# Where the loads of weights are issued: ScalarE beside its cast, or SyncE among the DMA transposes

## The chip, the cores and the metric

One core of one Trainium2 chip runs the kernel. The metric is the device time of one execution in microseconds (us), as the median of several. The engines are TensorE (PE), VectorE (DVE), ScalarE (ACT), GpSimd (POOL) and SyncE (SP); each has its own instruction queue and they meet by semaphores. DMAs are issued by SP, ACT or POOL on a queue of their own and carried out by 16 DMA engines that all of them share.

## The reference

Two layers over 256 tokens of width 1024, in float32:

```python
for l in range(2):
    x = x + 0.5 * swiglu_ffn(rmsnorm(x, norm_ffn1[l]), w_ffn1_in[l], w_ffn1_out[l])   # 2816 hidden
    u = rmsnorm(x, norm_mix[l])
    q, k, v, g, p, c, gates = split(u @ w_in[l])
    y_ret = (retention(q, k, v, positions) * silu(g)) @ w_ret_out[l]
    y_pool = pool_mixer(p, w_pool[l], pool_scale[l])
    y_conv = conv_module(c, ...)            # causal depthwise convolution, 31 taps
    x = x + (sig(g0) * y_ret + sig(g1) * y_pool + sig(g2) * y_conv) @ w_out[l]
    x = x + 0.5 * swiglu_ffn(rmsnorm(x, norm_ffn2[l]), w_ffn2_in[l], w_ffn2_out[l])
return rmsnorm(x, norm_final)
```

## The kernel before

Every product is made of three matmuls on numbers split in two: a high part (`w_hi`, rounded by a cast to fp32r) and a low part (`w_lo`, the rest). The weights come in one stream of 208 **halves** of 128 partitions x 2048 floats (1 MB; a few are smaller), two to a block, 104 to a layer, in the order in which TensorE uses them. For each half: a load into one of `RAWS` = 7 buffers `raw`; ScalarE's cast into one of `HIGHS` = 5 buffers `w_hi` (`cast`, L761 to L771); VectorE's subtraction into `w_lo`, which has the place of `raw` (`sub`, L1167, L1172); then the matmuls. TensorE says when a half is used up (`front_used`, `mm_done`), and `wait_half_used` (L340) waits for that: `cast(hf)` for half hf - 5, the load of hf for half hf - 7. So the load of half hf + 2 waits for the same half as the cast of hf.

SyncE runs one list for all halves (L713 to L735): wait until half hf - 7 is used, issue the load (L717), then, at fixed places, issue DMA transposes: `turn_h` (L672) for the hidden values of a feed-forward block, `turn_x` (L680) for x, `turn_qk` and `turn_ret` (L697) in the mixer. Each first waits for the 16-bit planes that ScalarE splits off (`split_h`, `split_x` L792) and for the buffer. A wait of SyncE holds what stands behind it in the list.

Between the parts lie five **seams** (`seam`, L840 on ScalarE, L1253 on VectorE): into the mixer and into the second feed-forward part of each layer, and into layer 1. There x is turned in four quarters, two for each 128 tokens. A quarter is added up (L1193), split (L796), turned (L684), joined by VectorE (`x_join`, L1210), scaled by ScalarE (`x_high`, L804) and its low part made by VectorE (`x_low`, L1219). ScalarE's order in a seam is: split quarter 1, square, split quarter 2, scale 1, `cast(hf + 1)`, `cast(hf + 2)`, scale 2, split 3, `cast(hf + 3)`, split 4, scale 3, square, scale 4, `cast(hf + 4)`. In the seam into the mixer of layer 0 hf is 34. SyncE has the first two transposes behind load hf + 2, the third behind hf + 3, the fourth behind hf + 4. In a mixer TensorE soon after turns `u` (`turn_u`, L484, L477), which VectorE makes in `gated_u` (L1345, L1348) after `sub` of half hf + 4.

In the mixer ScalarE splits the retention's result (`split_ret`, L936), SyncE turns it, ScalarE puts it together (`ret_out`, L943) and rounds it (`ret_high`), and TensorE waits for `ret_low`.

Of the kernel before, what the change touches and what calls it, by code (L numbers as in the profile page):

```python
# [15 lines left out]
P = 128  # L16
# [29 lines left out]
ALL_HALVES = L * HALVES  # L46
HALF_AT = 2048
HALF = P * HALF_AT
# [10 lines left out]
RAWS = 7  # L59
HIGHS = 5  # L60


FIRST = 4
# [44 lines left out]
def trunk(nc, x_in, positions, weights_in, gate_bias, pool_scale, norm_final, params, ident_in,  # L108
          inv_freq_in, decay_in, band_in, x_first_in, out):
    with ExitStack() as ctx:  # L110
# [3 lines left out]
        def sem(name):  # L114
            return ctx.enter_context(nc.semaphore(name))
# [43 lines left out]
        def place(name, shape, dt=F32):  # L159
            t = nc.alloc_sbuf_tensor_at(name, shape, dt, offset=end[0])  # L160
            end[0] += 4 * int(np.prod(shape[1:]))
            return t

        raw = place("raw", [P, RAWS, HALF_AT])
# [65 lines left out]
        raw_landed = [sem(f"raw_landed{i}") for i in range(RAWS)]  # L230
# [102 lines left out]
        def loads(hf):  # L333

            return hf // RAWS + (hf % RAWS >= FIRST)

        def size(hf):
            return HALF_SIZE[hf // 2 % CHUNKS]

        def wait_half_used(e, hf):  # L340


            l, g, second = hf // HALVES, hf // 2 % CHUNKS, hf % 2
            if g == M_POOL:
                e.wait_ge(mm_done, PRODUCT[l, g, 1, second])
            elif second:
                e.wait_ge(mm_done, PRODUCT[l, g, 1, 1 if (l, g, 1, 1) in PRODUCT else 0])
            else:
                e.wait_ge(front_used, l * (CHUNKS - 1) + g + (g < M_POOL))
# [11 lines left out]
        def wait_tr_taken(e, name):  # L361
            e.wait_ge(tr_taken[TURN[name] % 2], TURN[name] // 2 + 1)

        block = ctx.enter_context(nc.Block())

        @block.tensor
# [304 lines left out]
        def _(sp):  # L671
            def turn_h(l, f, b):  # L672
                at = (2 * l + f) * FB + b
                sp.wait_ge(h_split, T * (at + 1))
                sp.wait_ge(h_whole, at)
                sp.dma_start_transpose(hT_planes[:].rearrange("p a (g n) -> p (a g) n", n=P),
                                       h_planes[:].rearrange("p a k t n -> p (a k t n)")
                                       ).then_inc(h_turned, 16)

            def turn_x(l, norm, t, c):  # L680
                at = piece(l, norm, t, c)
                sp.wait_ge(x_split, at + 1)
                sp.wait_ge(x_joined, at)
                sp.dma_start_transpose(xT_planes[:].rearrange("p a (g n) -> p (a g) n", n=P),  # L684
                                       x_planes.rearrange("p a k n -> p (a k n)")
                                       ).then_inc(x_turned, 16)
# [13 lines left out]
                                       ret_planes[:, t].rearrange("p a h n -> p (a h n)")  # L700
                                       ).then_inc(ret_turned[t], 16)

            def half_in(hf):
                return weights_in[hf * HALF:(hf + 1) * HALF].rearrange("(p n) -> p n", p=P)

            for i in range(QUARTERS):
                s = columns(i % 4)
                sp.dma_start(raw[:, i // 4, s], half_in(i // 4)[:, s]  # L708
# [1 line left out]
            for t in range(T):  # L710
                sp.dma_start(x[:, t, :], x_in.rearrange("a (t p) d -> p (a t) d", p=P)[:, t, :]
                             ).then_inc(x_landed[t], 16)
            for hf in range(FIRST, ALL_HALVES):  # L713
                if hf >= RAWS:
                    wait_half_used(sp, hf - RAWS)
                n = size(hf)
                sp.dma_start(raw[:, hf % RAWS, 0:n], half_in(hf)[:, 0:n]  # L717
                             ).then_inc(raw_landed[hf % RAWS], 16)

                for at, norm in ((0, 0), (MIX, 1), (FFN2, 3)):  # L720
                    if (hf // HALVES, norm) in SEAM:
                        for ahead, t, c in ((2, 0, 0), (2, 0, 1), (3, 1, 0), (4, 1, 1)):
                            if hf % HALVES == 2 * at + ahead:
                                turn_x(hf // HALVES, norm, t, c)

                l, g = hf // HALVES, (hf % HALVES - RAWS - 1) // 2
                for f in (0, 1):
                    if hf % 2 == 0 and f * FFN2 <= g < f * FFN2 + FB:
                        turn_h(l, f, g - f * FFN2)
                for t in range(T):  # L730
                    if hf % HALVES == 2 * M_K + RAWS:
                        turn_qk(l, 0, t)
                    if hf % HALVES == 2 * M_V + RAWS:
                        turn_qk(l, 1, t)
                    if hf % HALVES == 2 * M_POOL + 1 + RAWS:  # L735
                        turn_ret(l, t)
# [7 lines left out]
        def _(act):  # L744
# [16 lines left out]
            def cast(hf):  # L761
                if hf >= ALL_HALVES:
                    return
                n = size(hf)
                act.wait_ge(raw_landed[hf % RAWS], 16 * loads(hf))
                if hf // 2 % CHUNKS == M_POOL:
                    act.wait_ge(pool_scaled, 2 * (hf // HALVES) + hf % 2 + 1)
                if hf >= HIGHS:
                    wait_half_used(act, hf - HIGHS)
                nc.scalar.copy(w_hi[:, hf % HIGHS, 0:n], raw[:, hf % RAWS, 0:n]  # L770
                               ).then_inc(hi_split, 1)  # L771

# [1095 lines left out]
```

## Time and profile before

| | us |
|---|---|
| median of 3 runs (1141.49 to 1142.49) | 1141.62 |
| the profiled execution | 1143.67 |
| its span | 1141.7 |
| busy: PE / DVE / ACT / POOL | 1128.9 / 794.9 / 630.0 / 31.5 |
| share of the span: PE / DVE / ACT | 99% / 70% / 55% |
| a load of 1 MB, issue to landing, median of 192 | 5.0 |
| a DMA transpose of x or the hidden values, issue to landing, median of 64 | 3.1 |

The spans and times below belong to the one profiled execution; the median is that of other executions. "Busy" of PE is modelled, since its matmuls overlap: a matmul of 512 columns is given 0.39 us there and the next one begins 0.23 us after it. The granted clock of TensorE is at full speed in all 40 slices of the page but for short stretches inside them.

### The profile page before, as it was taken

How to read it: one execution, taken by the hardware profiler on the slowest of the kernel's cores; microseconds unless marked ns; L12 is line 12 of the kernel's file. 1: busy time of each engine (PE TensorE's matmuls, PEld its weight loads, DVE VectorE, ACT ScalarE, POOL GpSimd, SP SyncE). 2: the span in 40 equal slices, each digit the busy share in tenths (PEclk: the TensorE clock that was granted, in tenths of full speed). 3: DMA queues.
4: the chain of work that ended last, by engine and by line, in shares of the span. 5: the costliest groups of instructions: out<-in, count | busy, mean ns of one | idle time of the engine just before them, and what ended most of it. 6: DMA issues, size and time to landing. Idle time of an engine off the chain costs nothing.

```text
span 1141.7 us, 13153 instructions
## 1 busy us (share of the span) xinstructions
PE 1128.9 (99%) x5063; PEld 931.9 (82%) x5063; DVE 794.9 (70%) x974; ACT 630.0 (55%) x723; POOL 31.5 (3%) x68
## 2 busy tenths in 40 slices
PE   9999999999999999999999999999999999999997
PEld 6788888788878888888888888878888788888886
DVE  5756565799999766555476656477999986665543
ACT  6755536654555675644465554275637366655442
POOL 1000000000100000000000000000001001000000
PEclk9999999999999999999999999999999999999999
DMA  9976665663764586756587656475637646876541
GB/s 348 324 242 219 211 233 160 239 175 139 243 241 151 164 292 212 238 156 230 174 274 250 236 180 233 176 217 207 212 120 261 233 152 184 273 244 210 168 184 37
DMA packets 116078, 240.99 MB, mean 211 GB/s; under 512 B 84256, under 2 KB 85664, under 8 KB 91440
## 3 DMA queue, kind: packets, MB, share of 16 engines
q1 hardware_dynamic: 112512, 232.28, 60.8%
q0 software_dynamic: 1648, 6.06, 1.5%
q10 hardware_dynamic: 1856, 1.81, 0.5%
q8 instruction: 40, 0.66, 0.2%
q14 instruction: 22, 0.18, 0.0%
HBM read 219.16 MB, written 1.05 MB: 193 GB/s over the span
## 4 chain that ended last, share of the span: by engine, by line
PE 86%; DVE 7%; DMA 2%; ACT 2%; issue 2%; SPq 1%; POOLq 0%; DVEq 0%; POOL 0%; ACTq 0%
PE acc L385 28%; PE acc L387 28%; PE acc L386 28%; DVE w_lo L1172 3%; DVE y L1396 1%; DMA raw<-in_weights 1%; PE tr L477 1%; ACT w_hi L770 1%; DMA hT_planes<-h_planes 1%; SPq L708 1%; ACT pin L945 0%; DVE gates L1471 0%; DVE ua L1452 0%; DVE gates L1416 0%; DVE qk L1461 0%
## 5 line engine op out<-in xcount | busy, mean ns | idle before, releaser
L1172 DVE TENSOR_TENSOR w_lo<-raw,w_hi 128x2048 fp32r<-128x2048 f32 (+2 forms) x204 | 444.4, 2211 | 87.7 <-ACT w_hi L770 87.7
L770 ACT CAST w_hi<-raw 128x2048 fp32r<-128x2048 f32 (+2 forms) x204 | 375.2, 1849 | 230.0 <-PE acc L387 221.8
L385 PE MATMUL acc<-w_hi,xT_hi 128*128 128x512 f32 x1152 | 453.1, 393 | 1.3 <-DVE w_lo L1172 1.1
L387 PE MATMUL acc<-w_hi,xT_lo 128*128 128x512 f32 x1152 | 449.3, 390 | 0.0
L386 PE MATMUL acc<-w_lo,xT_hi 128*128 128x512 f32 x1152 | 449.1, 390 | 0.0
L385 PEld LDWEIGHTS acc<-w_hi,xT_hi 128*128 128x128 f32 x1152 | 216.7, 188 | 46.4 <-DVE w_lo L1172 1.5
L387 PEld LDWEIGHTS acc<-w_hi,xT_lo 128*128 128x128 f32 x1152 | 216.7, 188 | 45.6
L386 PEld LDWEIGHTS acc<-w_lo,xT_hi 128*128 128x128 f32 x1152 | 216.9, 188 | 43.9
L1248 DVE SCALAR_TENSOR_TENSOR h<-acc,rs,silu_gate 128x256 f32<-128x256 f32 x88 | 42.5, 483 | 154.7 <-ACT silu_gate L837 154.4
L385 PE MATMUL acc<-w_hi,hT_hi 128*128 128x512 f32 x348 | 135.4, 389 | 0.0
L386 PE MATMUL acc<-w_lo,hT_hi 128*128 128x512 f32 x348 | 135.4, 389 | 0.0
L387 PE MATMUL acc<-w_hi,hT_lo 128*128 128x512 f32 x348 | 135.4, 389 | 0.0
L837 ACT ACTIVATE silu_gate<-acc,rs 128x256 f32<-128x256 f32 x88 | 41.6, 473 | 103.1 <-PE acc L387 103.1
L1396 DVE SCALAR_TENSOR_TENSOR y<-uT,par,y 128x256 f32<-128x256 f32 x240 | 97.2, 480 | 0.0
L386 PEld LDWEIGHTS acc<-w_lo,hT_hi 128*128 128x128 f32 x348 | 65.3, 188 | 13.7
L385 PEld LDWEIGHTS acc<-w_hi,hT_hi 128*128 128x128 f32 x348 | 65.3, 188 | 13.6
L387 PEld LDWEIGHTS acc<-w_hi,hT_lo 128*128 128x128 f32 x348 | 65.3, 188 | 13.4
L822 ACT COPY h_planes<-h 128x512 uint16<-128x512 uint16 x88 | 50.4, 620 | 8.9 <-DVE h L1248 8.9
L796 ACT COPY h_planes<-x 128x1024 uint16<-128x1024 uint16 x20 | 20.9, 1047 | 39.8 <-DVE x L1193 25.1
L1219 DVE SCALAR_TENSOR_TENSOR xT_lo<-hT_whole,par,xT_hi 128x128 fp32r<-128x128 f32 x80 | 22.7, 346 | 21.3 <-ACT xT_hi L804 21.3
L1231 DVE COPY hT_whole<-hT_planes 128x1024 uint16<-128x1024 uint16 x44 | 33.3, 757 | 5.8 <-DMA hT_planes<-h_planes 5.8
L804 ACT ACTIVATE xT_hi<-hT_whole,par 128x128 fp32r<-128x128 f32 x80 | 25.6, 392 | 15.4 <-DVE hT_whole L1210 15.4
(138 smaller groups left out, 629.4 us busy)
## 6 DMA issues: line engine op xcount, KB each, us to landing
raw<-in_weights SPq DMA_DIRECT2D x192, 1024.0 KB, 5.0
raw<-in_weights SPq DMA_DIRECT2D x20, 256.0 KB, 7.2
raw<-in_weights SPq DMA_DIRECT2D x8, 512.0 KB, 3.5
bias<-in_gate_bias POOLq DMA_DIRECT2D x6, 512.0 KB, 6.5
x<-in_x SPq DMA_DIRECT2D x2, 512.0 KB, 10.7
hT_planes<-h_planes SPq DMA_TRANSPOSE x64, 3.1
scale_row<-in_pool_scale POOLq DMA_DIRECT2D x2, 512.0 KB, 7.7
x_first<-in_x_first ACTq DMA_DIRECT2D x7, 128.0 KB, 6.0
```

What stands on the lines that cost most here:

```text
L385: nc.tensor.matmul(o, a_hi, b_hi, start=first, stop=False)
L386: nc.tensor.matmul(o, a_hi, b_lo, start=False, stop=False)
L387: return nc.tensor.matmul(o, a_lo, b_hi, start=False, stop=last)
L770: nc.scalar.copy(w_hi[:, hf % HIGHS, 0:n], raw[:, hf % RAWS, 0:n]).then_inc(hi_split, 1)
L804: nc.scalar.activation(xT_hi[:, k, tokens(t)], x_whole[:, i, :], ACT.Copy, scale=gain(l, norm, k)).then_inc(x_hi_ready, 1)
L822: nc.scalar.copy(h_planes[:, :, :, t, :], h[:, t, :].bitcast(U16).rearrange("p (k n a) -> p a k n", k=2, a=2)).then_inc(h_split, 1)
L837: nc.scalar.activation(silu_gate[:, t, :], acc[:, t, IN_BANK[g], 0:256], ACT.Silu, scale=rs[:, t:t + 1]).then_inc(silu_ready, 1)
L1172: nc.vector.tensor_tensor(w_lo[:, hf % RAWS, 0:n], raw[:, hf % RAWS, 0:n], w_hi[:, hf % HIGHS, 0:n].bitcast(F32), ALU.subtract).then_inc(l ...
L1219: a = nc.vector.scalar_tensor_tensor(xT_lo[:, k, tokens(t)], x_whole[:, i, :], gain(l, norm, k), xT_hi[:, k, tokens(t)].bitcast(F32), ALU. ...
L1231: nc.vector.tensor_copy(hT_whole[:].rearrange("p k n -> p (k n)").bitcast(U16) .rearrange("p (m a) -> p a m", a=2), hT_planes[:]).then_inc ...
L1248: nc.vector.scalar_tensor_tensor(h[:, t, :], acc[:, t, IN_BANK[g], 256:512], rs[:, t:t + 1], silu_gate[:, t, :], ALU.mult, ALU.mult).then_ ...
L1396: a = nc.vector.scalar_tensor_tensor(y[:, c, :], u, par[:, l, w:w + 1], y[:, c, :], ALU.mult, ALU.add)
```

## The change

ScalarE issues the loads of halves 7 to 207, each in `cast` of the half two before it, between the wait for the used half and the cast. The wait for the used half now stands ahead of those for the landed half and for the scaled pool weights. SyncE keeps the loads of halves 0 to 6, the transposes in their order, and no other wait.

```diff
+        def half_in(hf):
+            return weights_in[hf * HALF:(hf + 1) * HALF].rearrange("(p n) -> p n", p=P)
+
+        def load(e, hf):
+            n = size(hf)
+            e.dma_start(raw[:, hf % RAWS, 0:n], half_in(hf)[:, 0:n]
+                        ).then_inc(raw_landed[hf % RAWS], 16)
+
         block = ctx.enter_context(nc.Block())
...
-            for hf in range(FIRST, ALL_HALVES):
-                if hf >= RAWS:
-                    wait_half_used(sp, hf - RAWS)
-                n = size(hf)
-                sp.dma_start(raw[:, hf % RAWS, 0:n], half_in(hf)[:, 0:n]
-                             ).then_inc(raw_landed[hf % RAWS], 16)
+            for hf in range(FIRST, RAWS):
+                load(sp, hf)
+
+            for hf in range(RAWS, ALL_HALVES):
 
                 for at, norm in ((0, 0), (MIX, 1), (FFN2, 3)):
...
                 n = size(hf)
+                if hf >= HIGHS:
+
+                    wait_half_used(act, hf - HIGHS)
+                    if hf - HIGHS + RAWS < ALL_HALVES:
+                        load(act, hf - HIGHS + RAWS)
                 act.wait_ge(raw_landed[hf % RAWS], 16 * loads(hf))
                 if hf // 2 % CHUNKS == M_POOL:
                     act.wait_ge(pool_scaled, 2 * (hf // HALVES) + hf % 2 + 1)
-                if hf >= HIGHS:
-                    wait_half_used(act, hf - HIGHS)
                 nc.scalar.copy(w_hi[:, hf % HIGHS, 0:n], raw[:, hf % RAWS, 0:n]
                                ).then_inc(hi_split, 1)
```

## Rows read from the trace of the kernel before

**Rows 1.** The page, part 1: busy time, share of the span, instructions.

```profile
PE 1128.9 (99%) x5063; PEld 931.9 (82%) x5063; DVE 794.9 (70%) x974; ACT 630.0 (55%) x723; POOL 31.5 (3%) x68
```

**Rows 2.** Waits of PE: for whom, us in total, times, longest.

```profile
PE tr L477 <- issue: 2.3, 1, 2.3
...
PE acc L385 <- DVE w_lo L1172: 1.1, 1, 1.1
PE tr L477 <- DVE ua L1348: 0.9, 1, 0.9
```

**Rows 3.** The chain of waits in layer 0: start us, us, what.

```profile
203.07 2.29 issue
...
206.04 0.43 PE acc L385
```

**Rows 4.** Timeline of SyncE's queue, seam of layer 0: start, us, instruction.

```profile
176.46 5.40 SPq L684 DMA_TRANSPOSE hT_planes<-h_planes  x2
...
188.55 1.25 SPq L684 DMA_TRANSPOSE hT_planes<-h_planes  x1
...
194.23 1.24 SPq L684 DMA_TRANSPOSE hT_planes<-h_planes  x1
```

**Rows 5.** Timeline of ACT in the same seam, with idle time before.

```profile
181.69 3.70 ACT L770 CAST w_hi<-raw 128x2048 fp32r<-128x2048 f32 x2
...
191.68 1.05 ACT L796 COPY h_planes<-x 128x1024 uint16<-128x1024 uint16 x1 [1.34 <-DMA hT_planes<-h_planes]
...
199.26 1.89 ACT L770 CAST w_hi<-raw 128x2048 fp32r<-128x2048 f32 x1
```

**Rows 6.** Timeline of DVE in the same seam.

```profile
183.91 0.76 DVE L1210 COPY hT_whole<-hT_planes 128x1024 uint16<-128x1024 uint16 x1 [0.95 <-DMA hT_planes<-h_planes]
...
193.41 0.74 DVE L1210 COPY hT_whole<-hT_planes 128x1024 uint16<-128x1024 uint16 x1
...
199.38 1.14 DVE L1219 SCALAR_TENSOR_TENSOR xT_lo<-hT_whole,par,xT_hi 128x128 fp32r<-128x128 f32 x4 [1.35 <-ACT xT_hi L804]
201.18 2.29 DVE L1172 TENSOR_TENSOR w_lo<-raw,w_hi 128x2048 fp32r<-128x2048 f32 x1 [0.66 <-ACT w_hi L770]
```

**Rows 7.** Timeline of ACT and its DMA queue (ACTq) near the start.

```profile
4.57 0.33 ACTq L753 DMA_DIRECT2D x_first<-in_x_first  x1
4.98 0.60 ACT L777 CAST w_hi<-raw 128x512 fp32r<-128x512 f32 x1
```

**Rows 8.** Timeline of SyncE's queue in a feed-forward part.

```profile
114.71 3.05 SPq L717 DMA_DIRECT2D raw<-in_weights  x2
119.97 1.24 SPq L676 DMA_TRANSPOSE hT_planes<-h_planes  x1
```

**Rows 9.** DMA queues, 22 to 26 us (q1 SyncE's, q10 ScalarE's): packets, MB, share.

```profile
q1 hardware_dynamic: 210, 1.51, 90.7%
q10 hardware_dynamic: 209, 0.13, 10.9%
```

**Rows 10.** DMA queues from 121.8 to 122.7 us (q0 is GpSimd's).

```profile
q0 software_dynamic: 88, 0.36, 104.2%
q1 hardware_dynamic: 1, 0.00, 0.1%
```

**Rows 11.** The line of x's transposes (L684, 20 of them).

```profile
DMA to landing us min/median/max: 3.0/3.0/3.3
```

**Rows 12.** Timeline of PE: first matmul on the last quarter of x.

```profile
201.55 0.39 PE L385 MATMUL acc<-w_hi,xT_hi 128*128 128x512 f32 x1
```

**Rows 13.** Timeline of ACT near the start.

```profile
27.71 1.91 ACT L770 CAST w_hi<-raw 128x2048 fp32r<-128x2048 f32 x1 [2.02 <-DMA raw<-in_weights]
```

**Rows 14.** Timeline of SyncE's queue and of ACT, retention transposes of layer 0.

```profile
306.93 5.83 SPq L699 DMA_TRANSPOSE retT_planes<-ret_planes  x2
...
312.81 1.05 SPq L717 DMA_DIRECT2D raw<-in_weights  x2
...
314.64 1.35 ACT L945 COPY pin<-retT_planes 128x1024 uint16<-128x1024 uint16 x1
```

More of the change, by code:

```diff
@@ L701, in turn_ret @@
                                        ).then_inc(ret_turned[t], 16)
-            def half_in(hf):
-                return weights_in[hf * HALF:(hf + 1) * HALF].rearrange("(p n) -> p n", p=P)
             for i in range(QUARTERS):
```

## The prediction

> **What bounds the kernel now.** I read the page first, for the engine that is never idle. TensorE is: busy 99% of the span [rows 1]. Its waits come next, since only what adds to them can cost time and only what they hold can be gained. In all they are a few us [rows 2]: 2.3 before the turning of `u` in layer 0, 0.9 at the same place of layer 1, 1.1 near the start, and, too short for that view, four of 0.2 to 0.3 in the two mixers, where matmul starts lie 0.45 to 0.48 us apart. The chain of waits shows what the first does besides: after 2.29 us without work the matmuls come 0.43 us apart instead of 0.23 (1.2 instead of 2.4 GHz), nine of them [rows 3], which is 9 x 0.2 = 1.8 us. So some 8 us is all that any change to the waits could give back, and the question is what the new order adds.
>
> Then I followed that first wait back through the other engines. `gated_u` waits on VectorE behind `sub` of half 38 (201.18, 2.29 us), that behind ScalarE's cast (199.26), that behind the scaling of the last turned quarter, and so on through the four DMA transposes of the seam [rows 4, 5, 6]. The stretch from 183.91 to 194.15 is VectorE without a hole of more than 0.1 us, and it began when the second transpose landed. So a transpose that lands late moves the end of the kernel, us for us, at the seams that lead into a mixer. That is the place to examine.
>
> **The change part by part.** *Issues on ScalarE.* 201 loads (halves 7 to 207) leave SyncE for ScalarE. One takes 0.33 us of a queue, so 201 x 0.33 = 66 us of ScalarE's sequencer. ScalarE is 55% busy, and the issue does not hold its datapath: the issue at 4.57 stands behind the cast in the program and yet began 0.4 us before that cast ran at 4.98 [rows 7]. Where a copy or an activation is running (the casts at 181.69 and 199.26) the issue lies beneath it: 0 to 0.1 us. Where ScalarE was waiting for the half, the cast comes 0.33 us later; `sub` reads it some 2 to 4 us later in those stretches. I take 0.1 us on the path, at most 0.4. If the cover failed at the two seams, it would be 0.33 at each.
>
> *Time of the loads.* The same half is waited for, so in the feed-forward blocks a load leaves when it does now. There two loads are issued from 114.71 and the transpose only at 119.97, when most of their bytes are in [rows 8]; these blocks keep their distance. At the seams it is otherwise. Now SyncE issues load 37 behind the second transpose, 38 behind the third, 39 behind the fourth [rows 4]. After, 37 goes with `cast(35)`, at about 181.4, 38 with `cast(36)`, at 182.7 (half 31 used), and 39 with `cast(37)`, at about 187.5, under the splitting of `x` [rows 5]. The transposes are issued at 180.6, 188.55 and 194.23. So up to three loads of 1 MB (5.0 us each from issue to landing, some 2.5 us of it when they follow one another closely) are on the 16 DMA engines while the second and the third transpose want them, and from another queue, where order of issue protects nothing.
>
> *What a transpose loses there.* The trace has no transpose beside ScalarE's queue. Two kinds of rows bound it. Two plain transfers on two queues share one for one: 210 packets of SyncE's queue against 209 of ScalarE's between 22 and 26 us [rows 9]. A transpose beside another queue's transfer did worse: issued at 119.97 and ready some 1.2 us later, it moved one packet from 121.8 to 122.7 while GpSimd's load of `scale_row` moved 88 [rows 8, 10]; three more transposes of layer 0 show the same. Alone, a transpose takes 3.0 us [rows 11]. I go by the nearest row, that one: a transpose that finds a load in progress waits until the loads are through. For the second transpose it is less clear, since it is ready at 181.8 and load 37's first packets come at about 182.2: between 0 (it finishes first) and 5.5 us (it stands until loads 37 and 38 are through at about 189). I take 0.6. For the third: ready at 189.8, loads 38 and 39 through at about 192, then 1.8 us to landing, so 193.8 instead of 191.6. Splitting the last quarter on ScalarE (1.05 us, now at 191.68) then ends at 194.9, where SyncE now issues the fourth transpose at 194.23 after VectorE's joining [rows 4, 5, 6]: another 0.7. That makes 1.3 us a seam.
>
> *What the seams cost.* At the two that lead into a mixer the whole 1.3 arrives: 2.6 us. At the other three no `u` is turned; TensorE first needs the last quarter, which is ready at 200.52 and read from 201.55 in the seam shown [rows 6, 12], a slack of 1.0 to 1.3 us: 0.1 us each, 0.3 in all. The wait in layer 1 grows from 1.3 us between matmul starts to 2.6, which is what the wait of layer 0 has (2.68); there the clock fell, at 1.3 it did not [rows 2, 3]. I add 1.7 us for it, with 0 as the other end.
>
> The Trainium skill would have it milder (DMA: Bandwidth & Descriptors, section on queues, rings and completion order): a DMA engine goes round the queues packet by packet and drains a whole packet, typically 9 to 17 descriptors, before it switches. By that the 64 rows that a transpose has on each engine would be held up some five times by one 8 KB row. The rows on `scale_row` speak against it. At 0.31 us a row that would be an estimate of 1.5 us for the second transpose and, the third having slack, nearly the same sum.
>
> *The start.* Loads 7 and 8 are issued on SyncE's queue right behind 4 to 6 now. After, 7 leaves ScalarE when it comes to `cast(5)`, at about 25.4, and shares one for one with the tail of load 5, for which ScalarE waits until 27.71 [rows 13]. That cast releases the activation, `hidden` and `sub` of half 5 that end TensorE's 1.1 us wait. Between 0 and 1.2 us; I take 1.0, since at 22 to 26 us the sharing was one for one.
>
> *The retention transposes.* Issued from 306.93, now behind loads 59 and 60 on the one queue; ScalarE reads the first at 314.64 [rows 14], when VectorE lets it, and TensorE waits 0.2 us for what follows. After, load 61 leaves at 310.4 instead of 312.81 and can get in before the second: 0 to 2.4 us a layer. I take 0.5 each, 1.0 in all.
>
> Sum: 0.1 + 2.6 + 0.3 + 1.7 + 1.0 + 1.0 = 6.7 us. The profiled execution was 1143.67 us with a span of 1141.7, and the median of the runs is 1141.62; the sum goes on the median: **1148.0 us** (1148.3, rounded).
>
> **The rivals.** *Hidden.* A transpose loses only what the sharing takes from it, load 37 comes too late to touch the second, and the third has its slack of 1.5 us (191.6 landed against 193.41 read). Then the seams give 0.1, the start 0.5, the rest nothing: 1141.6 + 0.6 = 1142.2, within the bound. It decides from the point at which the second transpose has sent its rows before load 37's arrive, some 0.4 us at issue. For it speaks that the issues are hidden; against it the `scale_row` row. The Trainium skill stands on its side (same page, section Issuing engines are not separate DMA queues): starting DMAs from several engines saves only the sequencer's time, the transfers interleave. Chance 0.30.
>
> *Starved.* The second transpose also stands until its loads are through: 5.5 us at each of the two seams, 5.5 - 1.2 = 4.3 at each of the other three, 2.4 in each mixer, 1.2 at the start, and the clock falls after five or so new waits, 1.8 each: 11 + 13 + 5 + 1 + 9 = 39, about 1180 us. For it speaks that a transpose in progress has also stopped until the last of the 16 engines was free; against it that it would be 0.3 us ahead. Chance 0.20, with partial forms of it from 1155 on.
>
> *Faster.* Transposes no longer stand behind loads on their own queue, and at the start 5 and 6 have nothing behind them. The start's wait (1.3 us between matmul starts) and the four mixer waits of 0.2 to 0.3 would go: 1141.6 - 1.3 - 1.0 = 1139.3, at the edge of what can be told, or less if something unseen ties the loads to the path. The seams' transposes land in 3.0 us now, so nothing is to be had there. Chance 0.10, of which some ends within the bound.
>
> **How the numbers follow.** The forecast (a delay of 2.3 to 13 us) has 0.40. A measurement of this kernel can tell about 0.2%, 2.3 us, from no change. Faster 0.09, within 0.2% 0.31, slower 0.60. The range reaches down over the hidden case to 1140.5 and up into the starved one to 1168, leaving out about 0.07 below and 0.13 above.
>
> **What would show it.** In the profile after: the third transpose of a seam takes 5 us from issue to landing instead of 3.0 (starved: the second too, 6 to 8; hidden: both near 3); the wait before the turning of `u` in layer 1 is 2 us or more, with matmuls 0.43 us apart behind it; load 5 lands a us later; casts begin 0.33 us after the half is used where they waited for it, and without delay behind activations. I am wrong if transposes land in 3 us beside loads, or if ScalarE's datapath stands still during an issue.

## The result, and the profile after

The changed kernel took **1197.9 us** (median of 4 runs, 1195.7 to 1205.1) against 1141.7 of the kernel before: a ratio of 1.050, 95% interval 1.048 to 1.052. The forecast was 1148.0 with a range up to 1168. The sign was right, and the size was not: 56.3 us where I had summed 6.7.

The profiled execution took 1195.67 us with a span of 1193.8. The page after, in its parts 1, 4, 5 and 6:

```profile
PE 1145.4 (96%) x5063; PEld 937.5 (79%) x5063; DVE 792.6 (66%) x974; ACT 625.7 (52%) x723; POOL 31.8 (3%) x68
...
DMA hT_planes<-h_planes 20%; PE acc L393 20%; PE acc L395 19%; PE acc L394 19%; DVE w_lo L1178 3%; DMA retT_planes<-ret_planes 3%; DMA raw<-in_weights 2%; ACT h_planes L802 2%; ACT w_hi L776 2%; ACT h_planes L828 1%; PE tr L485 1%; SPq L713 1%; DVE hT_whole L1216 1%; DVE x L1199 0%; ACT xT_hi L810 0%
...
L828 ACT COPY h_planes<-h 128x512 uint16<-128x512 uint16 x88 | 50.4, 617 | 167.8 <-DMA hT_planes<-h_planes 158.9
...
hT_planes<-h_planes SPq DMA_TRANSPOSE x64, 6.3
```

VectorE's and ScalarE's work has not grown. What has is the time of a transfer: transposes are 23% of the chain of work that ended last (20 and 3, in its second line), their median time to landing is 6.3 us, and ScalarE waits 159 us for them ahead of its copies of `h_planes`. For TensorE the waits are these (for whom, us in total, times, longest):

```profile
PE acc L393 <- DVE sideT_lo L1434: 16.2, 2, 11.1
PE acc L393 <- DVE w_lo L1178: 11.9, 8, 5.0
PE acc L393 <- DVE xT_lo L1225: 6.5, 9, 0.9
PE tr L485 <- issue: 3.1, 1, 3.1
PE tr L485 <- DVE ua L1354: 2.0, 1, 2.0
PE acc L435 <- ACT w_hi L783: 1.6, 2, 0.9
PE ret L669 <- DVE scale_row L1168: 1.2, 1, 1.2
```

They add up to 42.5 us. The same view of the kernel before gives 6.7, so the waits grew by 35.8 us. PE's busy time grew from 1128.9 [rows 1] to 1145.4, 16.5 us, for the same 5063 matmuls. Together that is 52.3, and the spans differ by 52.1; busy and idle time always add up to the span, so this only says that nothing is missing. The second part is modelled time. About half of it is the clock: in the trace after, 50 of the large matmuls begin 0.40 to 0.47 us after the one before, in the trace before 9, and 41 x 0.2 us is 8 us. The other half isn't broken down; waits so short that the modelled 0.39 us of a matmul covers them are part of it. Behind the longest wait the matmuls start 0.43 us apart, and the granted clock there is half (columns of the second fence: the stretch, its length, busy time and instructions of PE, PEld, DVE, ACT and POOL, PEclk, DMA share, GB/s):

```profile
351.27 0.79 PE L393 MATMUL acc<-w_hi,sideT_hi 128*128 128x512 f32 x1 [11.07 <-DVE sideT_lo L1434]
351.86 0.63 PE L394 MATMUL acc<-w_lo,sideT_hi 128*128 128x512 f32 x1
352.29 0.63 PE L395 MATMUL acc<-w_hi,sideT_lo 128*128 128x512 f32 x1
```

```profile
351.30:354.30 3.00, 3.00 (x7) 2.42 (x8) 3.00 (x8) 1.78 (x1) 0.00 (x0) 0.50 0.97 347
```

Three kinds of transposes, by their lines (the feed-forward blocks' L684, `x`'s at the seams L692, retention's L707). Before, `x`'s had 3.0/3.0/3.3 [rows 11]. The landing times before of the blocks' (L676) and of retention's (L699) were these:

```profile
DMA to landing us min/median/max: 3.0/3.1/5.9
```

```profile
DMA to landing us min/median/max: 5.4/6.4/7.1
```

And after:

```profile
L684 SPq DMA_TRANSPOSE hT_planes<-h_planes x44: 1232/1323/2382, 33.3 to 1131.5; - x44
...
DMA to landing us min/median/max: 3.0/8.3/16.4
```

```profile
L692 SPq DMA_TRANSPOSE hT_planes<-h_planes x20: 1232/1233/1571, 188.3 to 1014.9; - x20
...
DMA to landing us min/median/max: 3.0/4.0/6.5
```

```profile
L707 SPq DMA_TRANSPOSE retT_planes<-ret_planes x4: 1578/2826/3397, 323.3 to 913.1; - x4
...
DMA to landing us min/median/max: 6.8/10.0/18.2
```

The fourth kind, q's and k's, 8 in all, is as before: 3.0 to 6.2 us.

The feed-forward blocks, for which I had forecast nothing at all, are the worst in number. ScalarE's timeline shows how two of them go:

```profile
488.45 1.14 ACT L828 COPY h_planes<-h 128x512 uint16<-128x512 uint16 x2 [4.83 <-DMA hT_planes<-h_planes]
489.21 0.34 ACTq L369 DMA_DIRECT2D raw<-in_weights  x1
...
490.90 0.34 ACTq L369 DMA_DIRECT2D raw<-in_weights  x1
...
501.36 1.14 ACT L828 COPY h_planes<-h 128x512 uint16<-128x512 uint16 x2 [6.89 <-DMA hT_planes<-h_planes]
```

The copies split the block that is to be turned, and SyncE issues its transpose when both are done, at 489.62. ScalarE has issued a load 0.4 us before and issues another 1.3 us behind. The transpose lands after 11.7 us and the second load after 12.0. Because ScalarE's next split waits for that landing, its whole program is late by the time of the transpose, and its next loads again surround the next transpose. This reading, that the delay makes its own repetition, is tested below (e3, e8, e10).

And the queues are not merely busy meanwhile. The second retention transpose of layer 0 was issued at 325.67 and took 18.2 us; a load of ScalarE's, issued at 326.64, took 17.3. The DMA view from 331 to 341 us (first line: mean busy share of the 16 engines in 40 slices; then packets by queue, q10 ScalarE's and q1 SyncE's, with MB and share of time):

```profile
DMA  9970999599909190000012202220121000001824
...
DMA packets 420, 0.65 MB, mean 65 GB/s; under 512 B 351, under 2 KB 351, under 8 KB 351
...
q10 hardware_dynamic: 76, 0.57, 53.7%
```

In 10 us 76 rows of 8 KB moved. They took 53.7% of 16 x 10 us, that is 1.1 us each, and for half of the stretch the engines were nearly idle although both transfers were unfinished. Neither "one transfer waits for the other" nor "they share" describes this.

### The profile page after: what moved, and what is told of

Read it like the earlier page. It is cut to its first block, busy times and chain, and to the rows that moved or that the text cites. A ratio compares the mean times of both kernels' runs of the same rounds, so it can differ in the third digit from the quotient of the medians.

```text
span 1193.8 us, 12956 instructions
## 1 busy us (share of the span) xinstructions
PE 1145.4 (96%) x5063; PEld 937.5 (79%) x5063; DVE 792.6 (66%) x974; ACT 625.7 (52%) x723; POOL 31.8 (3%) x68
## 4 chain that ended last, share of the span: by engine, by line
PE 61%; DMA 25%; ACT 6%; DVE 5%; issue 2%; SPq 1%; ACTq 0%; POOLq 0%; POOL 0%; DVEq 0%
DMA hT_planes<-h_planes 20%; PE acc L393 20%; PE acc L395 19%; PE acc L394 19%; DVE w_lo L1178 3%; DMA retT_planes<-ret_planes 3%; DMA raw<-in_weights 2%; ACT h_planes L802 2%; ACT w_hi L776 2%; ACT h_planes L828 1%; PE tr L485 1%; SPq L713 1%; DVE hT_whole L1216 1%; DVE x L1199 0%; ACT xT_hi L810 0%
## 5 line engine op out<-in xcount | busy, mean ns | idle before, releaser
L393 PEld LDWEIGHTS acc<-w_hi,xT_hi 128*128 128x128 f32 x1152 | 218.0, 189 | 72.2 <-DVE w_lo L1178 15.5
L393 PEld LDWEIGHTS acc<-w_hi,hT_hi 128*128 128x128 f32 x348 | 65.3, 188 | 14.6 <-DVE w_lo L1178 0.9
L843 ACT ACTIVATE silu_gate<-acc,rs 128x256 f32<-128x256 f32 x88 | 41.4, 470 | 19.4 <-PE acc L395 19.4
L802 ACT COPY h_planes<-x 128x1024 uint16<-128x1024 uint16 x20 | 20.9, 1046 | 52.3 <-DVE x L1199 28.2
L393 PE MATMUL acc<-w_hi,sideT_hi 128*128 128x512 f32 (+1 forms) x80 | 32.3, 404 | 16.2 <-DVE sideT_lo L1434 16.2
```

The lines of the kernel that those rows point to most:

```text
L393: nc.tensor.matmul(o, a_hi, b_hi, start=first, stop=False)
L802: nc.scalar.copy(x_planes, x[:, t, columns(c)].bitcast(U16) .rearrange("p (k n a) -> p a k n", k=4, a=2)).then_inc(x_split, 1)
L843: nc.scalar.activation(silu_gate[:, t, :], acc[:, t, IN_BANK[g], 0:256], ACT.Silu, scale=rs[:, t:t + 1]).then_inc(silu_ready, 1)
```

## The experiments

### Two queues, or ScalarE?

Four kernels came first: one that measures transposes beside loads by themselves, one that puts loads and transposes both on ScalarE's queue, one that exchanges them (transposes begun by ScalarE, loads by SyncE as before), and one that leaves all transfers as they were and adds ScalarE's new waits and 201 issues, of 8 KB each.

**e1, one load ahead of or behind a transpose.** The decoder is left out; each case is timed three times in one execution.

```
SyncE:    wait(step 3); transpose(turned, planes)            # 256 KB
ScalarE:  wait(step 2); load(load_a, 1 MB)                   # other cases: 2 loads, 4 of 256 KB,
                                                             # at the same step, 1 us later; from SyncE or GpSimd
```

> This kernel leaves the whole decoder out: it copies x to the output and times single transfers, three times each, with nothing else running. A DMA transpose of 256 KB issued by SyncE: alone; about 1.5 us behind a 1 MB load on SyncE's own queue; about 1.5 us behind one or two 1 MB loads on ScalarE's queue, behind the same load in four pieces of 2 KB rows, behind a load on GpSimd's queue; and ahead of a load on ScalarE's queue, issued at the same time, about 1.5 us later, and a quarter as large. Theory 'two streams' (a transpose and a stream of rows on two queues hold each other up): alone 3.0 us; behind on the own queue it lands some 1.5 to 2 us after the load, which keeps its 5.0 us; on two queues the transpose takes 5 us or more, more than the load's rest plus 2 us, and the load itself takes clearly longer than 5.0. Theory 'only waiting' (the transpose waits for the load and nothing is lost): on two queues the pair ends as it does on one. Theory 'ScalarE' (the queue does not matter, the place on ScalarE does): every transpose about 3 us, every load about 5 us.

Alone the transpose lands after 3.1 us. Its line 1 us behind a load on its own queue, and then 1 us behind a load on ScalarE's:

```profile
L94 SPq DMA_TRANSPOSE turned<-planes x3: 1237/1238/1239, 24.3 to 41.2; - x3
...
DMA to landing us min/median/max: 5.2/5.3/5.4
...
L97 SPq DMA_TRANSPOSE turned<-planes x3: 1232/1232/1233, 49.5 to 66.4; - x3
...
DMA to landing us min/median/max: 5.4/5.4/5.5
```

The further medians: behind two loads of ScalarE's 7.8; with four short loads around it 8.4; behind GpSimd's load 6.2; load and transpose issued at the same moment 6.4; a load 1.0 us after the transpose 3.2, of 1 MB or of 256 KB. So a load ahead of a transpose delays it equally on either queue, until it is through, as I had taken it from the `scale_row` row [rows 10]. A load that comes 1 us behind a transpose which nothing delays does no harm. But no case gave 8 to 18 us with a single load, and a single load of a hardware queue itself kept 5.2 to 5.5 us, where the theory 'two streams' wanted it clearly longer. Something of the kernel was not yet in this study.

**e2, both on ScalarE's queue.**

```
-            for hf in range(RAWS, ALL_HALVES):  # SyncE; its transposes, shortened here
-                                turn_x(hf // HALVES, norm, t, c)
...
+                turn_x(act, l, norm, t, c)      # ScalarE, in split_x; likewise for h, q/k, retention
```

> The kernel after, with the transposes too issued by ScalarE, each right behind the copy that it needs, so that loads and transposes share one queue again, ScalarE's. Theory 'two streams': the collisions are gone although every load is still begun by ScalarE at the place of the change; 1142 to 1155 us, the excess from 76 issues of 1.24 us on ScalarE. Theory 'ScalarE' (its order and its issues delay loads and casts): no better than after, 1190 us or more, since it has more to issue and more to wait for.

1159.1 us (ratio 1.0147, 1.0132 to 1.0162), 4 us above the range expected. All loads are still ScalarE's, and 39 of the 56 us are gone. The 44 feed-forward transposes go back to 3.1 us:

```profile
L376 ACTq DMA_TRANSPOSE hT_planes<-h_planes x44: 1253/1254/2020, 33.0 to 1094.3; - x44
...
DMA to landing us min/median/max: 3.1/3.1/6.4
```

What stays, 16 us, is of another kind: TensorE waits ten times for `xT_lo` (6.4 us in all, twice at each of the five seams). By the program that is where ScalarE, to begin a transpose, first waits for VectorE to have taken the one before, and its casts stand behind that; it wasn't tried apart.

**e3, exchanged.**

```
-                                turn_x(hf // HALVES, norm, t, c)    # SyncE, between its loads
...
+                turn_x(act, l, norm, t, c)      # ScalarE; the loads stay with SyncE, issued when a half is used
```

> The kernel before (loads on SyncE, in its order, ScalarE's cast as it was) with the transposes alone moved to ScalarE, placed as in the run before. Loads and transposes stand on two queues, and no load is begun by ScalarE. Theory 'two streams': slow, 1165 to 1210 us, with transposes of the feed-forward parts taking 5 us and more. Theory 'ScalarE': about the kernel before, 1142 to 1150 us, since no load waits for ScalarE.

1187.9 us (ratio 1.0394, 1.0377 to 1.0411). It differs from e2 in the queue and the place of the loads, and is 29 us slower. ScalarE issues no load here, and at retention the stalls are back: these transposes take 6.2 to 21.2 us, and TensorE waits 19.4 us for `sideT_lo`.

```profile
L391 ACTq DMA_TRANSPOSE retT_planes<-ret_planes x4: 1278/2013/3415, 314.6 to 898.9; - x4
...
DMA to landing us min/median/max: 6.2/9.9/21.2
```

One part of what was expected did not come. The transposes of the feed-forward blocks were to take 5 us and more; in the profiled run their median is 3.1 (at most 8.6), and those much over 5 us stand at the head of a stretch. So two queues alone do not spoil these blocks. Here SyncE issues a load when a half is used, whether ScalarE is late or not, so the loop read above cannot close.

**e4, the issues alone.**

```
+                if hf >= HIGHS:
+                    wait_half_used(act, hf - HIGHS)
+                    act.dma_start(bit[:, k], half_in(hf)[:, 0:16])     # 8 KB; the loads stay with SyncE
```

> The kernel before, where ScalarE, at the place of the change in each cast, issues a transfer of 8 KB (64 bytes for each partition) that nobody reads; the wait for the used half stands ahead of it as in the change. It has ScalarE's 201 issues and the new order of the waits without the moved loads. Theory 'two streams': 1141 to 1144 us. Theory 'ScalarE': a good part of the 56 us, 1160 us or more (201 x 0.33 = 66 us at most).

1143.4 us against 1142.9: ratio 1.0007, 0.9998 to 1.0017. ScalarE's 201 issues and the earlier wait cost nothing that can be measured. From e2 to e4 together: most of the loss is not ScalarE's time, and not which engine begins the transposes; it needs transposes and loads in different queues.

### Where the 56 us are

In the next four kernels ScalarE begins only some of the loads; SyncE issues the others at their old place. With `by_act(hf)` true for the halves of one kind of stretch:

```
+                if not by_act(hf):
+                    wait_half_used(sp, hf - RAWS)
+                    load(sp, hf)
...
-                    if hf - HIGHS + RAWS < ALL_HALVES:
+                    if hf - HIGHS + RAWS < ALL_HALVES and by_act(hf - HIGHS + RAWS):
```

> ScalarE begins only the 20 loads that wait for halves of the last two chunks ahead of the five joints (seams) between feed-forward and mixer stretches; SyncE issues the other 181 in their old order. Theory 'two streams, place by place' (a load on one queue beside a transpose on the other costs where the two meet, and nowhere else): the seams alone carry the 13 us that they carry in the changed kernel (2 to 4 us at each of five), so 1150 to 1158 us; the second and third transposes of a seam take 5 to 6.5 and 5 us from issue to landing, the transposes of the feed-forward blocks and of retention 3.0 to 3.3. Rival 'it needs the whole stream on ScalarE' (loads issued late one after another keep the collisions going, a single seam recovers): within 4 us of the kernel before, 1141 to 1146. My forecast on record took 3 us for these.

> ScalarE begins only the 64 loads that wait for halves of the inner 16 chunks of each mixer; SyncE the other 137. Place by place: the second retention transpose still takes 13 to 18 us, with waits of TensorE of 5 to 11 us before what follows, so 1152 to 1160 us; the first of the two waits may vanish if a slightly different moment of issue avoids the meeting, then 1145 to 1152. Rival 'needs the whole stream': 1141 to 1146. My forecast on record took 1.0 us for these.

> ScalarE begins only the 117 loads that wait for halves of the feed-forward stretches (all but their last two chunks); SyncE the other 84. My forecast on record took 0 for these, since loads and transposes 'keep their distance': that would give 1141 to 1144 us, with transposes at 3.0 us. Place by place, from where the changed kernel falls behind (12 us in the first stretch, some 25 in the four): 1160 to 1170 us, with the blocks' transposes at 8 to 16 us each. If the excesses of the seams, mixers and feed-forward alone add up to the 56 us of the whole change (within 8), the places are independent; if they add to much less, they feed one another.

> As the feed-forward-only kernel, but ScalarE begins only the loads that wait for halves of the blocks 4 and later of each feed-forward stretch (85 loads), so that each stretch begins from the undisturbed state of the kernel before, and the crowded start of the program is SyncE's alone. Theory 'the meeting makes itself' (ScalarE issues a load as soon as its own wait for the landing of the last turned block ends, which is when the next block is ready to be turned): the slow transposes of 8 to 16 us come back within two blocks, 1150 to 1165 us. Rival 'only kept alive' (a meeting at the start of a stretch delays ScalarE, and the delay makes the next meeting; from a clean state loads and transposes keep their 5 us distance): transposes at 3.0 us and 1141 to 1144 us.

| kernel | loads of ScalarE | us | ratio, 95% interval | over before (1141.9) | my forecast for it |
|---|---|---|---|---|---|
| e5 seams | 20 | 1158.5 | 1.0142 (1.0127 to 1.0157) | 16.7 | 4.6, with the clock |
| e6 mixers | 64 | 1154.1 | 1.0092 (1.0070 to 1.0114) | 12.2 | 1.0 |
| e7 feed-forward | 117 | 1172.1 | 1.0260 (1.0208 to 1.0312) | 30.2 | 0 (and 1.0 for the start) |
| e8 feed-forward, later blocks | 85 of these | 1142.8 | 1.0005 (0.9996 to 1.0014) | 0.9 | 0 |

The first three add up to 59.1, against 56.3 of the whole change. The interval of e7 alone is 6 us wide on either side, so within that **the places add**, and the loss of each is there with the other two undone. Half is in the feed-forward stretches. e5 and e7 came out somewhat above what was expected of them. The runs of e6 and e7 scatter more than those of before (1149.8 to 1159.7 and 1164.0 to 1179.4 us), and the profiled run is the slowest of its four in both; of e10, below, it is the fastest.

e8 is the surprise, and speaks against my theory that the meeting makes itself from nothing. Without the first four blocks of each stretch the other 85 loads cost nothing, and the transposes of the blocks are as before. The lines of the blocks' transposes, first in e7, then in e8:

```profile
L693 SPq DMA_TRANSPOSE hT_planes<-h_planes x44: 1232/1308/2623, 32.3 to 1115.1; - x44
...
DMA to landing us min/median/max: 3.0/6.0/19.8
```

```profile
L693 SPq DMA_TRANSPOSE hT_planes<-h_planes x44: 1232/1236/2513, 32.8 to 1077.4; - x44
...
DMA to landing us min/median/max: 3.0/3.1/5.8
```

Midway in a stretch of e8 loads are issued at 468.38 and 476.45, the transpose between them at 471.73: 3.4 us behind one load and 4.7 ahead of the next.

```profile
468.38 0.33 ACTq L369 DMA_DIRECT2D raw<-in_weights  x1
...
476.45 0.34 ACTq L369 DMA_DIRECT2D raw<-in_weights  x1
```

That is the distance of which my forecast spoke. It exists, and holds as long as nothing disturbs it. At the head of a stretch it is disturbed: in layer 1 of e7 a load leaves at 613.62, with two more still under way, the transpose at 614.25, a load at 614.64, and the transpose needs 19.8 us.

What disturbs it could be read from the two traces. In the kernel before, at the head of the second stretch, SyncE issues the transpose first and the two loads behind it; the transpose lands after 3.0 us:

```profile
415.94 1.24 SPq L676 DMA_TRANSPOSE hT_planes<-h_planes  x1
417.23 1.06 SPq L717 DMA_DIRECT2D raw<-in_weights  x2
```

In the changed kernel ScalarE issues the same two loads while it still splits the block, 0.6 us ahead of the transpose at 448.30, and that one lands after 8.9 us:

```profile
447.66 0.82 ACTq L369 DMA_DIRECT2D raw<-in_weights  x2
```

So here a load does not leave when it did: on SyncE's list it had stood behind the transpose.

**e10, the other half of e8.** It has `by_act` true for blocks 0 to 3 only.

```
-            return ffn and b >= 4
+            return ffn and b < 4
```

> The other half of the kernel with the later blocks: ScalarE begins only the loads that wait for halves of the blocks 0 to 3 of each feed-forward stretch (32 of the 201), SyncE all others in their old order. If the loss of the feed-forward stretches (30 us with all 117 loads, 1 us with the 85 later ones) starts in the first blocks and is then kept alive, the slow transposes stand in blocks 0 to 3 or 4 only and the time is 10 to 22 us over the kernel before: 1152 to 1164. If it needs both (a start here and ScalarE's loads afterwards to be harmful), 1142 to 1150. If 'later blocks are free' was luck of that kernel and not their clean start, the two halves would not differ so much: under 1146.

1166.4 us (ratio 1.0219, 1.0192 to 1.0246), 23.5 more than before and 2 above the range expected: 32 loads cost nearly what all 117 cost. In the profiled run blocks 0 to 2 of every stretch have transposes of 8.1 to 16.6 us, and from block 3 on, SyncE's queue having the loads again, they are at 3 to 5. So the state is entered in the first blocks and left where the loads go back. In e7 it goes on for 3 to 10 blocks of a stretch and then ends by itself. That this is the other 7 us of e7 fits, but the intervals of e7 and e10 overlap.

### What stops a transpose

In the changed kernel 31 of the 44 block transposes take over 7.5 us. 27 of these had a load ahead *and* one behind. The other four, the first of each stretch, had only loads ahead, three of them, and took 8.5 to 9.8 us; e1 has 7.8 for two. What went beyond 10 us had a load behind it. **e9** measures that by itself, each case three times in one execution.

```
ScalarE:  wait(step 2); load(load_a)
SyncE:    wait(step 3); transpose(turned, planes)      # 0.5 us later
ScalarE:  wait(step 6); load(load_b)                   # 2.0 us after the first
```

> No decoder: its whole computation is left out, the output is the input copied, and the total time means nothing. A transpose of 256 KB as in the kernel, begun by SyncE, with 1 MB loads around it, each case three times, VectorE's steps of 0.42 us setting the moments. The first study of this kind had one load ahead of the transpose on either queue: 5.3 us on the same queue, 5.4 on the other, so that case alone does not explain 8 to 19 us. Theory 'jam' (a load that comes on the other queue behind a transpose which is itself behind a load stops both): load at 0, transpose at 0.4, load at 1.7 us gives 9 to 13 us for the transpose and about the same for the second load; the same three on SyncE's queue give 5.5 to 6 and 7.5 to 8; with a plain transfer of 256 KB in place of the transpose, or with the second load at 5 us, nothing is stopped (4 to 6 us, second load 7 or 5). Rival 'only queued' (a transpose waits for all loads that are on the other queue when it becomes ready, and the loads go at their full rate): 6.5 to 8 us for the transpose and no load over 7.7, in every case with loads of ScalarE. Halves (512 KB, rows of 4 KB) tell whether the length of the rows matters: the jam with it 7 us or more, the queue 4.5 to 5.5.

The lines of the transposes of two cases: loads on ScalarE's queue as above, and the same three on SyncE's queue. In the table, "late" is a second load issued only when the first has landed, 5.6 us behind the transpose.

```profile
L87 SPq DMA_TRANSPOSE turned<-planes x3: 1232/1241/1242, 28.8 to 53.0; - x3
...
DMA to landing us min/median/max: 8.6/8.6/9.1
...
L92 SPq DMA_TRANSPOSE turned<-planes x3: 1237/1237/1242, 64.7 to 85.0; - x3
...
DMA to landing us min/median/max: 6.0/6.0/6.0
```

All cases, medians of three:

| case | transpose | last load |
|---|---|---|
| load, transpose, load; two queues | 8.6 | 8.5 |
| the same on one queue | 6.0 | 7.2 |
| two queues, second load late | 5.9 | 5.1 |
| two queues, second load 0.5 us behind the transpose | 13.3 | 14.6 |
| two loads, transpose, load | 10.0 | 8.2 |
| transpose, then two loads within 1 us | 10.3 | 9.2 |
| halves (512 KB) around it | 7.5 (5.7 to 8.2) | 7.3 |
| a plain load of 256 KB in place of the transpose | 5.2 | 6.6 |

The 8.6 (8.6 to 9.1) lies just under what the jam was to give (9 to 13), above "only queued" (up to 8), and the case with the close second load, where queueing allows 8, gave 12.7 to 14.6. Queueing also asked for no load over 7.7 us, and in four cases it took 8.2 to 14.6. A plain transfer in the transpose's place is not stopped, nor stops the load. From the first issue to the last landing, the three transfers of the case with the close second load (94.6 to 110.3 us) went at 150 GB/s; three on one queue (84.4 to 93.6 us) at 256.

```profile
DMA packets 1344, 2.36 MB, mean 150 GB/s; under 512 B 1088, under 2 KB 1088, under 8 KB 1088
```

```profile
DMA packets 1344, 2.36 MB, mean 256 GB/s; under 512 B 1088, under 2 KB 1088, under 8 KB 1088
```

**e11, a guard.** If it is the load begun behind a waiting transpose that does it, holding that load back should be enough.

```
                 nc.scalar.copy(w_hi[:, hf % HIGHS, 0:n], ...)
+                if hf >= HIGHS and hf - HIGHS + RAWS < ALL_HALVES:
+                    for landed, count in turning.items():      # transposes whose split ScalarE has done
+                        act.wait_ge(landed, 16 * count)
+                    turning.clear()
+                    load(act, hf - HIGHS + RAWS)
```

> All 201 loads on ScalarE as in the changed kernel, but each is issued behind its cast and only when the transposes that ScalarE's own splits have led to so far (of h, x and the retention planes) have landed: no load can come behind a waiting transpose any more, while a load in progress ahead of one stays possible. Theory 'jam': the long stalls (8 to 19 us) go, what is left is 5 to 6 us transposes and later casts: 1143 to 1162 us, well below the changed kernel's 1198. Rival 'only queued, loads ahead do it': little changes, 1175 to 1200. Rival 'ScalarE's waits are the cost': slower than the changed kernel, over 1200, since it waits more.

1148.7 us (ratio 1.0053, 1.0039 to 1.0066). All 201 loads are ScalarE's, it waits more than in the changed kernel, and 49 of the 56 us are gone. No transpose of a block takes over 7.2 us:

```profile
L686 SPq DMA_TRANSPOSE hT_planes<-h_planes x44: 1232/1234/2849, 32.9 to 1084.0; - x44
...
DMA to landing us min/median/max: 3.0/3.9/7.2
```

So the loss goes when ScalarE's loads no longer surround a transpose. For the blocks this is not the load behind alone: the issue now stands behind the cast and the wait, and with it the last load ahead of a block's transpose has moved from 0.4 us before it to 2.4 us or more. Which of the two did more isn't separated there. The second retention transpose of layer 0 separates them better. In e6 it has loads of ScalarE's 7.9 and 7.1 us ahead of it and one 1.0 us behind, and takes 15.5 us; in e11 it has two 7.8 and 4.9 us ahead, none behind, and takes 5.5.

### A version that is faster than both

**e12.** The same reading of the profile said what could be gained: TensorE waits for `u` behind a half that nobody needs yet [rows 2, 3, 6]. In the seam into a mixer the cast and `sub` of the fourth half move behind the first blocks of `u`; transfers stay as before.

```
-                cast(hf + 4)                    # end of the seam, ScalarE; VectorE: sub(hf + 4)
+                if norm != 1:
+                    cast(hf + 4)
...
+                cast(ahead(M_A))                # mixer, behind the first take(M_B); VectorE: behind gated_u(l, 0)
```

> The kernel before with one thing changed in the joint that leads into a mixer: ScalarE's cast and VectorE's subtraction of the half that comes fourth there stand behind the first blocks of u instead of ahead of them (loads and transposes as before, all on SyncE's queue). It is a test of what the profile of before says bounds it: TensorE's waits of 2.3 and 0.9 us for u, and nine matmuls at the low clock behind the first (1.8 us). If that reading is right, up to 5 us go: 1136.5 to 1140 us. If another chain is as late (the last turned quarter), 1140.5 to 1142.5. If the half is then missed by the matmuls that follow: up to 1145.

1138.1 us against 1142.9: ratio 0.9960, 0.9947 to 0.9972. The two waits for `u` are gone from TensorE's list, and so are the matmuls at the low clock (the granted clock from 196 to 206 us is 1.00, and it was 0.50 from 206 to 209 before). The wait for `w_lo` at the start, 1.1 us before, is missing in this profiled run too, and the edit has no part in that. The list:

```profile
PE ret L661 <- DVE scale_row L1164: 1.2, 1, 1.2
PE acc L427 <- ACT w_hi L777: 0.3, 1, 0.3
```

## Why the prediction was right and wrong

**What bounds the kernel: right.** TensorE and its few waits; e12 gained 4.8 us, which this reading allowed. The list of waits was not whole: the view of before also has 1.2 us for `w_hi` and 1.2 for `scale_row`, both in the first 13 us. They change nothing in the sum.

**Issues on ScalarE, 0.1 us: right.** e4: 0.5 us between the medians, and the interval includes none at all.

**The start, 1.0 us: wrong in sign, of no weight.** TensorE's wait for `w_lo` there is 0.3 us after, 1.1 before [rows 2].

**The third transpose of a seam, 5 us instead of 3.0: right.** It took 4.9 to 5.1. **The second, 0.6 us of delay: mis-sized.** The bounds were 0 and 5.5. In layer 0 it was issued at 192.52 and the load at 193.22, 0.7 us behind (I had worked out 0.8), and landed after 6.2 us: a delay of 3.2, in the other seams 2.4 to 3.4. e1 brackets the point from which it decides: 6.4 us with the load at the same moment, 3.2 with the load 1.0 us later. The estimate that I had worked out from the Trainium skill for this one (DMA: Bandwidth & Descriptors, section on queues, rings and completion order, by which a DMA engine goes round the queues packet by packet) was 1.5 us. It was nearer than my 0.6 and still half of what came.

**The seams, 4.6 us with the clock: too small by 12.** e5 gave 16.7. By the `sub` of the same halves, compared well ahead of and behind each seam in the profiled runs of before and e5, the two seams into a mixer lost 5.3 and 4.4 us where I had 1.3, close to the delays of their second and third transposes together. The other three, for which I had allowed 0.1 each because their last quarter has a slack of 1 us, lost 2.1 to 2.3 each: the slack was measured for one late transpose, and two came late. The 1.7 us for the clock in layer 1 did not come in the changed kernel. The wait there was 2.0 us, as forecast, but the granted clock behind it (811.5 to 814.5 us) was 1.00 and the matmuls 0.23 us apart.

**The retention transposes, 1.0 us, at most 4.8: wrong.** e6 gave 12.2. I had bounded them by one load that gets in before the second transpose and goes at its full rate, and never by both transfers standing. The load left where I had put it, 1.0 us behind the second transpose; that is harmless in e1, where nothing delays the transpose, and here it still stood behind two loads.

**The feed-forward blocks, 0: the step that failed.** It carried 30 of the 56 us (e7). The sentence was "in the feed-forward blocks a load leaves when it does now ... these blocks keep their distance". Two things were wrong in it. It took the rows at 114.71 and 119.97 [rows 8], late in a stretch, for all blocks; e8 shows that there they do keep it, and e10 that at the head of a stretch they don't. There the loads did not leave when they do now either, since SyncE's list had held them behind the transpose (417.23 against 415.94). And on one queue the distance did not matter: there a transpose stands behind a load and takes 5 to 6 us. On two queues a block's transpose took between 3 and 20 us, by the moment of issue. I asked for each load *when* it leaves, and not what happens if ScalarE is late by a few us, although the change tied the loads to the one engine that itself waits for the transposes to land. That tie closes a loop: late landing, late loads, which then surround the next transpose. e3, which lacks the tie, has the blocks at a median of 3.1 us on two queues.

**The rivals.** *Hidden* fell with the first trace; the rule of the Trainium skill that stood on its side (same page, Issuing engines are not separate DMA queues: transfers begun by several engines interleave, and only the sequencer's time is saved) fits the plain loads of [rows 9] and the 5.2 and 6.6 us of e9, and not a transpose between loads. *Starved* (about 1180) had the right direction and was still too mild: it let loads run at full rate while the transpose stood, and it had nothing for the feed-forward blocks. My range ended short of its centre.

**What stays open.** Why a transpose and rows of 8 KB on another queue stop each other is not shown; the rows of a trace name packets, not what they wait for. Rows of 4 KB gave 7.5 us (5.7 to 8.2) in place of 8.6, with half the bytes, which doesn't separate the length of rows from the amount. The plain transfer of e9 had rows of 2 KB from HBM, the transpose 1024 pieces of 256 bytes within SBUF; whether it is the turning that matters or the many small pieces wasn't tried.

## What to carry to other kernels

A queue is also an order: loads behind a transpose on the same queue did not get in its way (6.0 us in e9, against 5.9 with none behind), and moving one of them to another queue gives that up. Before splitting transfers that were in one queue, ask what is between the issue and the landing of each transpose at the moment when the issuing engine is *late*, not in the steady state; and if the engine that now issues is one that waits for such a landing, expect the delay to feed itself. Keep transposes and large loads on one queue, or let the load wait until the transpose has landed (e11), and look for gains where TensorE waits (e12).

## What the runs showed of the hardware

- A transpose of 256 KB (3.1 us alone) that is issued 1.0 us behind a 1 MB load needs 5.3 to 5.4 us, on the load's queue or on another (e1).
- With a second load begun on another queue 0.5 or 1.5 us behind it, both take 8.4 to 15.8 us in the isolated case (e9) and up to 20 in the kernel (e7); the 16 engines then stand nearly idle for whole us (65 GB/s from 331 to 341 us), and rows of 8 KB take 1.1 us each.
- At retention it occurs whichever of ScalarE and SyncE has the transposes (21.2 us in e3, 18.2 after). On one queue, ScalarE's too (at most 7.1 us in e2), it doesn't.
- A plain transfer of the same 256 KB between the same loads lands after 5.2 us (e9).
